# Differential attention: values of the first four heads projected with tokens in rows, ahead of queries and keys, at five or six k steps a tick

## What is computed

```
def diff_attn_mixer(h, w_in, lq1, lk1, lq2, lk2, subln, w_out, lambda_init):
    proj = h @ w_in                                   # q, k: 8 heads x 2 x 64; v, gate: 8 heads x 128
    q, k, v, gate = jnp.split(proj, [...], axis=-1)
    q = rope(q, cos, sin); k = rope(k, cos, sin)
    ...
        s = einsum('bhcqd,bhckd->bhcqk', qi, kt) * scale      # causal
        pr = softmax(s)
        att = pr[:, :, 0] - lam * pr[:, :, 1]
        return einsum('bhqk,bhkd->bhqd', att, vt)
    o = rms_norm(o, subln, DA_SUBLN_EPS) * (1.0 - lambda_init)
    return (o * jax.nn.silu(gate)) @ w_out
```

## Time and profile before

| | us |
|---|---|
| median of 3 runs | 1174.98 |
| lowest, highest | 1172.5, 1176.56 |
| the profiled execution | 1177.03 |
| its span, first to last instruction | 1175.0 |

### The profile page before, as it was taken

How to read it: one execution, slowest core, us unless ns; L and a number is a source line. 1 busy time by engine, 2 the same in 40 slices (tenths; PEclk the granted TensorE clock), 3 DMA queues, 4 the chain that set the end, 5 groups by cost and what they waited for, 6 DMA issues and landing times.

```text
span 1175.0 us, 19408 instructions
## 1 busy us (share of the span) xinstructions
PE 1135.0 (97%) x7558; PEld 887.5 (76%) x7558; DVE 735.1 (63%) x1166; ACT 608.7 (52%) x1026; POOL 464.7 (40%) x375
## 2 busy tenths in 40 slices
PE   6999989998999999999999999999999999999998
PEld 5756767777867887777777777878888888867776
DVE  6768986875666455766766475474494234557773
ACT  5867444634655456556665455463112334556563
POOL 2331023556743543333333245444544445433240
PEclk8999999999999999999999999999999999999999
DMA  8912347345073543221221222532333333321211
GB/s 268 284 54 72 81 109 215 108 135 125 9 253 119 161 124 90 72 73 55 72 72 55 73 76 89 177 90 78 102 90 107 90 99 99 90 73 56 71 54 72
DMA packets 194685, 123.02 MB, mean 105 GB/s; under 512 B 27878, under 2 KB 181031, under 8 KB 194215
## 3 DMA queue, kind: packets, MB, share of 16 engines
q1 hardware_dynamic: 191990, 119.27, 34.7%
q10 hardware_dynamic: 2608, 2.56, 0.6%
HBM read 105.03 MB, written 16.78 MB: 104 GB/s over the span
## 4 chain that ended last, share of the span: by engine, by line
PE 42%; issue 23%; POOL 12%; DVE 7%; ACT 1%; DMA 1%; POOLq 0%; ACTq 0%; DVEq 0%; SPq 0%
POOL b_w_lo L669 12%; PE banks L757 10%; PE banks L759 10%; PE banks L758 10%; DVE b_problems L2376 1%; DVE b_sum_squares L2374 1%; PE banks L1406 1%; PE banks L1013 1%; PE banks L764 1%; PE banks L1434 1%; DVE b_suffix L2859 1%; DVE b_a_lo L2207 1%; PE banks L1416 1%; PE banks L1032 1%; DMA b_problems<-d_a 1%
## 5 line engine op out<-in xcount | busy, mean ns | idle before, releaser
L669 POOL TENSOR_TENSOR b_w_lo<-b_w_raw,b_w_hi 128x512 fp32r<-128x512 f32 x296 | 398.0, 1365 | 650.3 <-ACT b_w_hi L1511 650.2
L757 PE MATMUL banks<-b_a_lo,b_w_hi 128*128 128x512 f32 x1232 | 498.3, 404 | 12.4 <-POOL b_w_lo L669 5.5
L759 PE MATMUL banks<-b_a_hi,b_w_lo 128*128 128x512 f32 x1232 | 482.9, 392 | 0.0
L758 PE MATMUL banks<-b_a_hi,b_w_hi 128*128 128x512 f32 x1232 | 482.3, 392 | 0.0
L1511 ACT ACTIVATE b_w_hi<-b_w_raw 128x1024 fp32r<-128x1024 f32 x156 | 165.0, 1057 | 262.0 <-PE banks L759 249.9
L757 PEld LDWEIGHTS banks<-b_a_lo,b_w_hi 128*128 128x128 f32 x1232 | 232.5, 189 | 78.2 <-issue 16.7
L759 PEld LDWEIGHTS banks<-b_a_hi,b_w_lo 128*128 128x128 f32 x1232 | 232.4, 189 | 50.6
L758 PEld LDWEIGHTS banks<-b_a_hi,b_w_hi 128*128 128x128 f32 x1232 | 232.8, 189 | 44.2 <-issue 0.5
L1946 ACT ACTIVATE b_exps<-banks,b_stats 128x128 f32<-128x128 f32 (+3 forms) x64 | 33.2, 524 | 58.3 <-DVE b_stats L2643 58.3
L2499 DVE SCALAR_TENSOR_TENSOR b_a_lo<-b_x_t,b_params,b_a_hi 128x512 fp32r<-128x512 f32 x32 | 35.6, 1125 | 23.6 <-ACT b_a_hi L1848 23.6
L2641 DVE TENSOR_TENSOR banks<-banks,b_consts 128x256 f32<-128x256 f32 x32 | 13.8, 432 | 46.3 <-PE banks L1262 45.2
(11 more groups left out here) (358 smaller groups left out, 1561.3 us busy)
## 6 DMA issues: line engine op xcount, KB each, us to landing
b_w_raw<-rw_w_in SPq DMA_DIRECT2D x32, 512.0 KB, 4.4
b_w_raw<-da_w_in SPq DMA_DIRECT2D x32, 512.0 KB, 4.0
b_w_raw<-w_in_a SPq DMA_DIRECT2D x32, 512.0 KB, 4.0
b_w_raw<-pe_w_gate SPq DMA_DIRECT2D x16, 512.0 KB, 4.1
d_ple<-b_ple_out SPq DMA_DIRECT2D x16, 256.0 KB, 4.3
b_w_raw<-rw_w_out SPq DMA_DIRECT2D x8, 512.0 KB, 4.1
b_ple_in<-d_ple SPq DMA_DIRECT2D x2, 2048.0 KB, 10.5
b_w_raw<-da_w_out SPq DMA_DIRECT2D x8, 512.0 KB, 3.9
```

What stands on the lines that cost most here:

```text
L669: m = pool.tensor_tensor(WLO[:, u % 2, ks], WRAW[:, u, ks], WHI[:, u % 2, ks].bitcast(F32), ALU.subtract)
L757: pe.matmul(dst, hi, a_lo[:, k_act, :], start=first, stop=False)
L758: pe.matmul(dst, hi, a_hi[:, k_act, :], start=False, stop=False)
L759: return pe.matmul(dst, lo, a_hi[:, k_act, :], start=False, stop=last)
```

## The change

The values of heads 0 to 3 are projected in one piece ahead of all else. The 4 slots that they take are now `("values", u)`: a slot holds two k blocks of 512 value columns (the load has rows of 2 KB where a block of 128 columns has rows of 512 B), and each k step is the product for one block of 128 tokens: tokens end up in partitions, so the activation is the stationary operand and the weights are streamed. The four token blocks accumulate in BANK[0], [1], [2] and [7] side by side over all 32 k steps. DVE scales them into DV (one instruction for each bank, L2673 of the new program), and `stage_v`, `turn_v` and `keep_v` remain for heads 4 to 7 only, at ticks 14, 20, 24 and 28 (DA_TURNS).

Then come q and k of heads 0 to 3, then q, k, v of heads 4 to 7, then the gates. scores(0) now stands after 48 k steps (slots 0 to 5), and the ticks hold 6 k steps for steps 0 to 3, 5 for steps 4 to 27, 6 for steps 28 to 31 (`da_at`), so that from step 28 on both programs have the same k step beside the same attention step.

```diff
+DA_SLOTS = [("values", u) for u in range(4)]
+DA_SLOTS += [(kind, j) for j in range(4) for kind in "qk"] + [(kind, j) for j in range(4, NT) for kind in "qkv"]
+DA_SLOTS += [("g", j) for j in range(NT)]
+DA_TURNS = (14, 20, 24, 28)
+def da_at(tick):
+    if tick <= 4:
+        return 48 + 6 * tick
+    return 72 + 5 * (tick - 4) if tick <= 28 else 192 + 6 * (tick - 28)
+def da_bank(i):
+    return 3 if i == 4 else (i - 5) % 3
+VALUE_BANKS = (0, 1, 2, 7)
...
+        def value_step(t, k, w_hi, w_lo):
+            a_hi, a_lo = (x[:, k, t * P:(t + 1) * P] for x in ACTS[0])
+            bank = BANK[VALUE_BANKS[t]]
+            pe.matmul(bank, a_lo, w_hi, start=(k == 0), stop=False)
+            pe.matmul(bank, a_hi, w_hi, start=False, stop=False)
+            return pe.matmul(bank, a_hi, w_lo, start=False, stop=(k == NT - 1))
...
-                    pe.wait_ge(sem("bank_free"), n0 + i - (3 if i < 3 else 2))
-                if i == 0:
-                    pe.wait_ge(sem("act_ready"), A_DA + k + 1)
-                m = split_product(BANK[i % 3], i % 2, lambda w, k=k: w[:, k, :], k, k == 0, k == NT - 1)
+                if i < 4:
+                    k2, t = k // TT, (3, 0, 1, 2)[k % TT]
+                    kt = 2 * i + k2
+                    if t == 3:
+                        pe.wait_ge(sem("act_ready"), A_DA + kt + 1)
+                    elif kt == 0:
+                        pe.wait_ge(sem("bank_free"), n0 - 3 + t)
+                    m = value_step(t, kt, *(flat(w[:, i % 2])[:, k2 * TOK:(k2 + 1) * TOK] for w in (WHI, WLO)))
...
-        for tick in range(DA_STEPS + 4):
-            if tick >= 4:
-                scores(tick - 4)
-            if tick >= 6:
-                values(tick - 6)
-            da_dense(6 * tick, 6 * tick + 3)
-            if tick >= 5:
-                turns(tick - 5)
-            if tick >= 4 and tick % 4 == 0:
-                turn_v(tick // 4 - 1)
-            da_dense(6 * tick + 3, 6 * tick + 6)
+        da_dense(0, da_at(0))
+        for tick in range(DA_STEPS):
+            scores(tick)
+            if tick >= 2:
+                values(tick - 2)
+            da_dense(da_at(tick), da_at(tick) + 3)
+            if tick >= 1:
+                turns(tick - 1)
+            if tick in DA_TURNS:
+                turn_v(DA_TURNS.index(tick))
+            da_dense(da_at(tick) + 3, da_at(tick + 1))
...
+        for u in range(3, 6):
+            hi(g0 + u)
+        rotate(0)
+        hi(g0 + 6)
+        rotate(1)
...
+        got(n0 + 3)
+        for t in range(TT):
+            ts(DV[:, t, 0:TOK], BANK[VALUE_BANKS[t]], NST[:, t:t + 1], None, ALU.mult).then_inc(sem("bank_free"), 1)
```

More of the change, by code:

```diff
@@ L125, with da_slot, da_tick @@
 DA_STEPS = NT * TT
+DA_SLOTS = [("values", u) for u in range(4)]
[6 more added lines that the diff above has]
+    return 72 + 5 * (tick - 4) if tick <= 28 else 192 + 6 * (tick - 28)
+def da_slot(kind, j):
+    return DA_SLOTS.index((kind, j))
+def da_bank(i):
+    return 3 if i == 4 else (i - 5) % 3
+def da_tick(i):
+    return next(tick for tick in range(DA_STEPS + 1) if da_at(tick) >= 8 * (i + 1))
+VALUE_BANKS = (0, 1, 2, 7)
 SB_SLOTS = [(kind, pair) for pair in range(4) for kind in "kqv"] + [("g", pair) for pair in range(4)]
@@ L141 @@
 OUT_BANKS = (2, 4, 0, 6)
-DAO_BANKS = (0, 2, 7, 3, 0, 1, 2, 3)
+DAO_BANKS = (0, 1, 7, 3, 0, 1, 2, 3)
 def build(nc, a, out):
@@ L1263, in scores, with turn_v @@
             m.then_inc(sem("score_mm"), 1)
-        def turn_v(j):
-            pe.wait_ge(sem("v_staged"), j + 1)
-            if j:
-                pe.wait_ge(sem("att_turned"), 4 * j - 1)
-            turn_four(BANK[5], [VSTAGE[:, j % 2, t * P:(t + 1) * P] for t in range(TT)]).then_inc(sem("v_mm"), 1)
+        def turn_v(n):
+            pe.wait_ge(sem("v_staged"), n + 1)
+            pe.wait_ge(sem("att_turned"), DA_TURNS[n] - 1)
+            turn_four(BANK[5], [VSTAGE[:, n % 2, t * P:(t + 1) * P] for t in range(TT)]).then_inc(sem("v_mm"), 1)
         def turns(s):
@@ L1277, in turns @@
                 pe.wait_ge(sem("att_turned"), s - 1)
-            pe.wait_ge(sem("v_turned"), j + 1)
+            turned = sum(tick <= s for tick in DA_TURNS)
+            if turned:
+                pe.wait_ge(sem("v_turned"), turned)
             for t in range(q + 1):
@@ L1918, in rotate @@
         def rotate(n):
-            j, which = divmod(n, 2)
-            act.wait_ge(sem("mm_done"), n0 + 3 * j + which + 1)
+            i = da_slot("qk"[n % 2], n // 2)
+            act.wait_ge(sem("mm_done"), n0 + i + 1)
             if n >= 2:
@@ L1925, in rotate @@
                 m = act.activation(rotated_tile(n)[32 * (q ^ 1):32 * (q ^ 1) + 32, :],
-                                   BANK[(3 * j + which) % 3][32 * q:32 * q + 32, :], ACT.Copy)
+                                   BANK[da_bank(i)][32 * q:32 * q + 32, :], ACT.Copy)
             m.then_inc(sem("rotated"), 1)
-        rotate(0)
         keep_rstd(RB[:, :], 3, BANK[4])
@@ L1956, in keep_att @@
             act.activation(ATTT[:, s % 2, 0:w], BANK[5 + s % 2][:, 0:w], ACT.Copy).then_inc(sem("att_turned"), 1)
-        for tick in range(DA_STEPS + 4):
-            p, q = divmod(tick, 4)
-            if q == 0 and p:
-                hi(g0 + 3 * p + 1)
-            if tick >= 4:
-                exps(tick - 4)
-            if tick >= 5:
-                keep_att(tick - 5)
-            if q == 0 and p:
-                keep_v(p - 1)
-            if q == 1 and p:
-                hi(g0 + 3 * p + 2)
-            if q == 2:
-                hi(g0 + 3 * p + 3)
-            if q in (1, 2) and p < NT and tick != 1:
-                rotate(2 * p + q - 1)
+        for tick in range(DA_STEPS):
+            freed = [i for i in range(7, 28) if da_at(tick) <= 8 * (i - 1) < da_at(tick + 1)]
+            for i in freed:
+                if 8 * (i - 1) == da_at(tick):
+                    hi(g0 + i)
+            exps(tick)
+            if tick >= 1:
+                keep_att(tick - 1)
+            if tick in DA_TURNS:
+                keep_v(DA_TURNS.index(tick))
+            for i in freed:
+                if 8 * (i - 1) > da_at(tick):
+                    hi(g0 + i)
+            for n in range(2, 2 * NT):
+                if da_tick(da_slot("qk"[n % 2], n // 2)) == tick + 1:
+                    rotate(n)
         def sub_square(j):
@@ L2659, in head_out @@
             dve.tensor_copy(DQT[:, j, :], BANK[7]).then_inc(sem("head_out"), 1)
-        for tick in range(DA_STEPS + 4):
-            p, q = divmod(tick, 4)
-            if q == 0 and p:
-                stage_v(p - 1)
-            if tick >= 4:
-                maxima(tick - 4)
-            if q in (2, 3) and 0 < p < NT:
-                rope(2 * p + q - 2)
-            if q == 1 and p >= 2:
-                head_out(p - 2)
-            if tick >= 4:
-                combine(tick - 4)
-            if p == NT and q >= 2:
-                raw_gate(q - 2)
+        for tick in range(DA_STEPS):
+            if tick in DA_TURNS:
+                stage_v(DA_TURNS.index(tick))
+            maxima(tick)
+            for n in range(2, 2 * NT):
+                if da_tick(da_slot("qk"[n % 2], n // 2)) == tick:
+                    rope(n)
+            if tick % TT == 1 and tick > TT:
+                head_out(tick // TT - 1)
+            combine(tick)
+            if tick >= DA_STEPS - 2:
+                raw_gate(tick - DA_STEPS + 2)
         SUBG = PRM[:, PARAM_ROWS + 1:PARAM_ROWS + 2]
```

44 lines of the change are left out of this document (29 added, 15 removed).

## The result

The changed kernel took 1180.34 us in the median of 20 runs (1175.4 to 1184.8), the kernel before 1176.38 us (1172.3 to 1182.6, also 20). The ratio is 1.0036, its 95% interval 1.0022 to 1.0050: slower by 0.36%, between 2.6 and 5.9 us. The forecast was 1.0034 and +4.0 us.

The account below looks back on a forecast made before the run. PE was taken to bound the kernel. Transposes -1.44, pitch -0.3, opening -0.2, wait +4.3 and clock fall +1.6 gave +4.0 us on 1174.98, so 1179.0 us (0.34% slower), with an 8-in-10 range of 1174.3 to 1183.

Parts of the forecast that it names:

- The wait: Before scores(0): PE idles until DVE ends key 0's rope, no slot lying between; 4.3 us, bounds 3.8 and 5.0.
- The chain without a meeting: Before scores(0): DVE's copies, cosine and sine products and sum after the key's slot, undisturbed by POOL; 3.8 us.
- the meeting with POOL: In key 0's rope: a DVE instruction is held up while POOL writes low weights; 0.55 us, at most 1.27.
- The clock behind it: Behind the wait at scores(0): PE's clock falls after the idle time; 1.6 us, bounds 0 to 2.8.
- The transposes: In the ticks of heads 0 to 3: four `turn_v` leave PE, 0.36 us each; -1.44 us.
- The opening: Ahead of the sums: PE's wait stays but changes from act_ready to acc_done; -0.2 us.
- The opening's fall: Behind the opening's idle time: a clock fall of about 1.6 us, taken to stay and left out of the sum.
- rival A: No clock fall behind the wait, or none at the opening: 1177.4 us; both: 1175.8 us; chance 0.28.
- Value slots and ticks: Value slots and five-step ticks cost nothing; ticks of 5.2, 5.3, 5.0 and 5.5 us, no scores waiting on exponentials.
- Rival B: In the five-step ticks: DVE becomes the bound, 12 ticks each missing by 0.5 us; +6, 1185 us; chance 0.10.
- pitch: 24 k steps move from ticks to the plain stretch before scores(0), where matmuls start 0.2267 us apart, not 0.23; -0.3 us.

Follow-up runs that it names:

- experiment 3: The changed kernel with ACT's rounding of slot 7's weights moved behind the first exponentials, so POOL is idle during the key's rope; 1179.7 us, ratio 1.0031.
- experiment 10: The changed kernel profiled once more with nothing edited; 1181.67 us in one run.
- experiment 6: The changed kernel with the sums of squares and the spread of the root four k steps later; 1180.61 us, ratio 1.0043.
- experiment 2: The changed kernel with 20 useless matmuls into an unread bank just ahead of scores(0); 1178.62 us, ratio 1.0017.
- experiment 4: The kernel before with only head 0's slots reordered to value, query, key, DVE and ACT orders to match; 1182.7 us, ratio 1.0061.
- experiment 1: The changed kernel with scores(0) moved from k step 48 to 55 and ticks 0 to 3 cut to 4, 4, 4, 5 k steps; 1176.49 us, ratio 1.0001.
- experiment 5: The changed kernel with scores(0) at k step 55, five-step ticks, slot 6's weights rounded earlier and sums four k steps later; 1175.38 us, ratio 0.9994.

## Why the prediction came out

**The wait: right in place, cause and releaser.** One idle of PE ahead of L1315, ended by DVE's L2664. Forecast 4.3 us, measured by starts 4.8: 497.43 less the end of the pitch in front of it. The chain without a meeting was right within 0.1: 3.8 forecast, 3.9 by starts in experiment 3 (492.67 less 488.55 and a pitch). Mis-sized was the meeting with POOL. I took 0.55 us from the one case in the earlier trace rows, bounds 0 to 1.27; it was 0.94.

The Trainium skill, page "SBUF — State Buffer", section "Who interferes with whom", says that such a pair of instructions shuts each other out for a whole instruction. The 0.94 us agree with it better than my 0.55 did, and POOL's pair took 3.40 us instead of the 2.54 of the earlier trace rows, so it loses as well here. By the full length the wait would have been 5.0; the runs show 4.8.

**The clock behind it: right that it falls, too short.** 1.6 us forecast, 2.76 measured, just within the bounds of 0 to 2.8 (experiment 10 has 2.87, just outside). I had chosen between the case with 1.6 and the case with 2.8 in the earlier trace rows the one that lay in the same stage; the case with the idle time most like the new one, 3.38 us, would have been nearer this time, though not for experiments 3 and 6, where the fall cost 1.5. The lower bound, nought, came from the 2.53 us of the earlier trace rows with the full clock behind them. That too was one execution: see the last section. That the fall belongs to the idle time and not to the slots or the banks is shown by experiment 2, where a busy PE keeps the clock (one profiled execution, against five of five that stood still and fell), and by experiment 4, where the kernel before gets it with the same wait.

**The transposes: 1.7 us instead of 1.44.** I had taken the distance from the group's start to the next matmul, 0.36 us, but the next matmul pays too. PE's timeline of after has two ticks of the same width and five k steps, the second with a `turn_v` (L800):

```profile
563.83 0.49 PE L1315 MATMUL banks<-b_dk_t,b_dq_t 64*128 64x128 f32 x4
569.01 0.70 PE L1315 MATMUL banks<-b_dk_t,b_dq_t 64*128 64x256 f32 x4
...
606.12 0.49 PE L1315 MATMUL banks<-b_dk_t,b_dq_t 64*128 64x128 f32 x4
609.82 0.60 PE L800 MATMUL banks<-b_consts,b_v_stage 128*128 128x128 f32 x4
```

The first lasts 569.01 − 563.83 = 5.18 us, the second 5.61; the difference is 0.43, times four 1.7. The pair at width 384 gives 5.38 less 4.96, about the same.

**The opening: −0.1 us where −0.2 stood.** The wait changed its name from act_ready to the squares, as the sum said, and lost 0.2 us, of which the sums behind it give back 0.1: they take 0.92 us to the next matmul instead of 0.80.

**The opening's fall: a wrong footing.** I took the fall in the earlier trace rows as the kernel's own and left its 1.6 us out as unchanged. It is absent in after, as one half of rival A had it. That can't be put down to the change, since the kernel before has it in only one of four executions; whether the change makes it rarer still, these few can't tell. Against the kernel's usual self the change costs 5.4 us in the stage, against the execution shown 3.9. The interval of the times, 2.6 to 5.9 us, allows both.

**Value slots and ticks: right.** A slot of values takes 5.44 us, eight k steps at the pitch of before. The five-step ticks take 5.18, 5.31, 4.96 and 5.51 us; 5.2, 5.3, 5.0 and 5.5 were forecast. No score waits for exponentials in after, the least spare is 0.57 us, at the width of 384, where I had worked out 1.1. Rival B therefore did not occur, but its mechanism did in experiments 1 and 5, at another alignment. I had priced it as a uniform lack of DVE time; what decides is which rope falls into which width, and whether POOL's pair falls on the same moment.

**The sum.** For the stage, against before's usual 186.49: +4.8 (wait) +2.76 (fall) −1.7 (transposes) −0.1 (opening) −0.3 (pitch, as forecast) = +5.5, and the table has +5.4. My terms were 4.3 + 1.6 − 1.44 − 0.2 − 0.3 = +4.0. Two terms on the costly side were too small by some 1.6 us together, one gain by 0.26. Against the execution that I had counted from, the stage lost 3.9 us, next to my 4.0, but only because that execution had a fall of 1.54 us at the opening that after did not: one error made up for the other, by luck. That the medians differ by 4.0 as well lies within their own spread and is no credit to the sum either; the direction and the mechanism are what the runs show.

**Not settled.** The fall costs 2.76, 2.29 and 2.87 us in three executions (after, experiments 4 and 10) and 1.55 and 1.53 in two (experiments 3 and 6), with much the same waits. How much of it passes before PE starts again accounts for the differences among the first three. Why the full clock is back so much earlier in the last two, no run explains; nor why the opening had a fall in one execution of four.

## What to carry over

When values, or any operand that is needed late, are projected first, look at which slot now ends right ahead of the first use of its own product. The work behind a projection (here a rope of 3.8 us on DVE) needs one slot of something else behind it: putting the key two slots earlier, with the sums later too (0.45 us in experiment 6), turned +0.36% into −0.20%. And when a stretch of one profiled execution, such as the opening's slow clock, carries a term of the sum, look for it in a second execution first.
